# One program instead of two phases: the projection and linear attention of tiles 1 to 8 run as steps beside the expert gathers, with input weights streamed per batch

## The reference, cut to what matters

```python
h = rmsnorm(x, g_norm1); z = h @ w_in
gq, gk, gv, gg, glr, fq, fk, fv, ff = jnp.split(z, _split_points(), axis=-1)
log_a = log_sigmoid(glr @ w_gla_a2 + b_gla_a) / 16
o_gla, S_new = gla_recurrence(gq, gk, gv, log_a, S0)      # linear attention, 4 heads
o_gla = rmsnorm(o_gla, g_gla_onorm) * silu(gg)
o_fox = fox_attention(rmsnorm(fq), k_all, v_all, c_all, P) # softmax attention, 8 heads
x = x + concat[o_gla, o_fox] @ w_out
h = rmsnorm(x, g_norm2)
# PEER: per token and head the best 16 of 128 x 128 experts by two sub-key scores
a = gelu(einsum('nhkd,nd->nhk', peer_u[idx], h))
x = x + einsum('nhk,nhkd->nd', softmax(top) * a, peer_v[idx])
```

## Time and profile before

| | us |
|---|---|
| median of 3 runs | 3622.26 |
| lowest and highest | 3621.23, 3624.48 |
| the profiled execution, span | 3627.2 |
| phase one, to the start of phase two | 0 to 610 |
| first dot product of a gathered row | 693.1 |
| last slots | 3618 |

### The profile page before, as it was taken

The page is one execution under the profiler, slowest core; times in us unless marked ns, Lnnn a source line. Parts: engine busy times, 40 slices in busy tenths (PEclk is TensorE's granted clock), DMA queues, the critical chain, the costliest instruction groups (busy, mean ns, idle before and its releaser), DMA issues.

```text
span 3627.2 us, 32138 instructions
## 1 busy us (share of the span) xinstructions
PE 2778.7 (77%) x8313; PEld 1424.2 (39%) x8313; DVE 2582.2 (71%) x5512; ACT 1483.7 (41%) x3893; POOL 1316.7 (36%) x1154
## 2 busy tenths in 40 slices
PE   7999996677777776777787777677777777787677
PEld 3444445434333343343344343333343333343333
DVE  4333332586886768897786899878777888876786
ACT  2333333244445534444452444444524443343344
POOL 0000001234434444344444444434444543444343
PEclk9999997788888888898888898889988998888889
DMA  4010125799999999999999999999999999999998
GB/s 193 24 47 24 47 100 205 274 420 407 421 399 409 421 421 403 370 413 404 414 420 421 421 408 408 352 421 422 421 421 420 407 414 401 398 404 409 422 420 352
DMA packets 187467, 1267.78 MB, mean 350 GB/s; under 512 B 23508, under 2 KB 24492, under 8 KB 39956
## 3 DMA queue, kind: packets, MB, share of 16 engines
q0 software_dynamic: 159728, 1131.10, 76.3%
q1 hardware_dynamic: 26356, 130.32, 9.0%
q10 hardware_dynamic: 1200, 4.33, 0.3%
HBM read 1238.78 MB, written 26.88 MB: 349 GB/s over the span
## 4 chain that ended last, share of the span: by engine, by line
DMA 33%; PE 20%; DVE 15%; issue 9%; ACT 4%; POOL 2%; DVEq 0%; SPq 0%; ACTq 0%; POOLq 0%
DMA w_in<-in_peer_uv,expert_index 33%; PE ps_acc L1530 13%; DVE w_in L1701 6%; DVE v_sums L1709 3%; PE ps_scores L1506 3%; POOL w_in L1193 2%; PE ps_scores L1386 1%; ACT coef_diag L1360 1%; PE ps_scores L1474 1%; ACT gelu_u_dot_h L1355 1%; DVE key_top_index L1608 1%; DVE key_scores_rest L1609 1%; PE ps_fox_o L1404 1%; DVE key_top_index L1617 1%; DVE expert_top_index L1608 1%
## 5 line engine op out<-in xcount | busy, mean ns | idle before, releaser
L1530 PE MATMUL ps_acc<-w_in,coef_diag 128*128 128x512 f32 x2676 | 1535.2, 716 | 733.0 <-ACT coef_diag L1360 708.2
L1193 POOL DMA_INDIRECT w_in<-in_peer_uv,expert_index x1056 | 1264.7, 1198 | 1667.1 <-PE ps_acc L1530 1466.9
L1701 DVE CUSTOM_DVE_ANT_0 w_in<-w_in 128x1024 f32<-128x1024 f32 x1056 | 1285.7, 1220 | 457.6 <-DMA w_in<-in_peer_uv,expert_index 448.0
L1530 PEld LDWEIGHTS ps_acc<-w_in,coef_diag 128*128 128x128 f32 x2676 | 558.5, 223 | 1514.1 <-ACT coef_diag L1360 972.1
L1355 ACT ACTIVATE gelu_u_dot_h<-u_dot_h 128x2 f32<-128x2 f32 x528 | 107.1, 203 | 1312.7 <-DVE u_dot_h L1701 1299.5
L1709 DVE SCALAR_TENSOR_TENSOR v_sums<-w_in,coefficients,v_sums 128x1024 f32<-128x1024 f32 x387 | 495.7, 1281 | 12.7 <-ACT coefficients L1362 12.3
L460 PE MATMUL ps_z<-w_in,x_T 128*128 128x512 f32 x864 | 407.7, 622 | 6.4 <-DVE w_in L782 6.4
L1506 PE MATMUL ps_scores<-w_in,rows_T 128*128 128x256 f32 x1152 | 263.1, 382 | 0.7 <-issue 0.7
L1360 ACT ACTIVATE coef_diag<-coef_diag,gelu_u_dot_h 128x128 f32<-128x128 f32 x669 | 253.1, 398 | 17.5
L1506 PEld LDWEIGHTS ps_scores<-w_in,rows_T 128*128 128x128 f32 x1152 | 221.2, 192 | 62.7 <-issue 35.7
L460 PEld LDWEIGHTS ps_z<-w_in,x_T 128*128 128x128 f32 x864 | 165.3, 199 | 194.5 <-issue 185.1
(11 more groups left out here) (200 smaller groups left out, 2353.2 us busy)
## 6 DMA issues: line engine op xcount, KB each, us to landing
w_in<-scratch_keys_w SPq DMA_DIRECT2D x48, 1024.0 KB
w_in<-in_w_out_chunks SPq DMA_DIRECT2D x24, 1024.0 KB
w_in<-in_peer_uv,expert_index POOLq DMA_INDIRECT x1056
w_in<-in_w_in_chunks SPq DMA_DIRECT2D x6, 2048.0 KB, 25.0
w_in<-in_w_peer_q_T SPq DMA_DIRECT2D x8, 1024.0 KB, 5.9
scratch_keys_w<-w_in SPq DMA_DIRECT2D x8, 1024.0 KB, 3.9
x_T<-in_x_T POOLq DMA_DIRECT2D x9, 512.0 KB, 4.5
x_rows<-in_x_rows POOLq DMA_DIRECT2D x9, 512.0 KB, 5.2
```

What stands on the lines that cost most here:

```text
L1193: pool.indirect_dma_start(out=ring[:, s % RING, :], out_offset=None, in_=dram["uv"], in_offset=bass.IndirectOffsetOnAxis(ap=idx[:, t % IDX ...
L1530: mm = pe.matmul(acc[:, c, :], diag[:, r, :], ring[:, r, D + c * 512:D + (c + 1) * 512], start=first, stop=False, skip_group_check=True)
L1701: dve.tensor_tensor_reduce(out=ring[:, s % RING, 0:D], in0=ring[:, s % RING, 0:D], in1=h2[:, t % 2, :], scale=1.0, scalar=0.0, op0=ALU.mul ...
```

## The change

The two functions become one, `stream`. Batches are 0, 1-2, 3-4, 5-6, 7-8. On each engine the front of a batch now begins with `mix_front` (projection of its tiles, two tiles to each weight chunk, and the gates) and `gla` (linear attention of one tile, 14 steps, 12 for the sample), ahead of `attend`. The rest of the front and the back stay, but for names.

- w_in is no longer kept. Its twelve half chunks of 256 columns (1 MB) are streamed in every batch, ahead of w_out's and keys_w's, through two buffers (`WBUF = 2`). g_norm1 is multiplied into the turned rows of x instead of into w_in.
- q, k, v, the gates and the linear attention's output stay in SBUF; k, v and log gates are stored as outputs by SyncE and no longer read back. One tile of 5440 columns is shared by linear attention, softmax attention and routing (GpSimd clears it once).
- Folding of the keys is 32 pieces, one in each step of tile 0's linear and softmax attention. Its results are stored in 16 halves; w_q lies in the ring meanwhile, so GpSimd waits for all foldings before the first gather.
- VectorE's copy of h is single: `reopen(t)` stands at the first slot of tile t, not four slots before.
- The front has 1799 steps (1551 before), 108 of them ahead of slot 0 (78). VectorE has 394 of the adds (387).
- The scratch for GpSimd's descriptors is 4096 bytes instead of the default.

`front_plan` gives the new steps the weights in the diff. The slots over which its table spreads a part:

| part | before | change |
|---|---|---|
| rest of routing 0 | 0-40 | 0-17 |
| projection of a batch's tiles | phase one | 18-55, 181-242, 419-479, 676-737 |
| linear attention of a batch | phase one | 55-67, 243-262, 480-500, 737-756 |
| attention 1; 2 | 41-59; 136-161 | 68-76; 76-87 |
| attention 4; 7; 8 | 346-386; 644-705; 875-949 | 287-314; 757-799; 800-845 |
| routing of two tiles | 232-344, 473-586, 744-873 | 104-181, 341-418, 599-676, 872-1040 |

```diff
+BATCHES = [[0], [1, 2], [3, 4], [5, 6], [7, 8]]
+NB = max(len(ts) for ts in BATCHES)
+PLACE = {t: (bi, i) for bi, ts in enumerate(BATCHES) for i, t in enumerate(ts)}
+CW = 2 * DKEY
+PAIRS = 6
+QK, VV, FK, FV, FQ, GG = range(PAIRS)
+IN_CH = 2 * PAIRS
+OUT_CH = D // CW
+CHUNKS = IN_CH + OUT_CH + PH
+WBUF = 2
...
-def mix_phase(nc, ctx, io, dram, shared):
...
+def gla_at(ts):
+    return len(ts) + 1 + IN_CH * len(ts) + 2
+
+
+def gla_steps(t):
+    return 7 + len(levels(t))
+
...
+def front_plan():
...
+    for ts in BATCHES:
+        n = len(ts)
+        weight += [0.6] * (n + 1) + [3.7] * (IN_CH * n) + [0.6] * 2
+        on_pe += [True] * gla_at(ts)
+        for t in ts:
+            weight += [1.1] * gla_steps(t)
+            on_pe += [False] * gla_steps(t)
+        for t in ts:
+            weight += [(13.0 + 7.5 * min(t, TILES - 0.5)) / ATT_STEPS] * ATT_STEPS
+        weight += [3.5] * (OUT_CH * n) + [1.5] * (out_steps(ts) - OUT_CH * n)
+        base = len(weight)
+        on_pe += [True] * (base - len(on_pe))
+        due += [(base, SLOTS * t - 12) for t in ts if t]
+        weight += [0.45] * route_steps(ts)
+        on_pe += [False] * route_steps(ts)
...
-BATCHES = [[0], [1], [2, 3], [4, 5], [6, 7], [8]]
...
-WBUF = 3
...
+        def turned_rows(bi, ts):
+            if bi:
+                sp.wait_ge(s_mm, units_before(bi))
+            for i, t in enumerate(ts):
+                sp.dma_start(xT[i][:].rearrange("p k t -> p (k t)"), dram["xT"][t]).then_inc(x_in[i], 16)
...
+                turned_rows(bi, ts)
+                sp.dma_start(g1[:], dram["g1"]).then_inc(g1_in, 16)
+                sp.dma_start(w_small[:].rearrange("p k n -> p (k n)"), dram["w_in_small"]).then_inc(g1_in, 16)
+                chunk(bi, 0)
+            else:
+                chunk(bi, 0)
+                turned_rows(bi, ts)
+            rows(bi, ts)
+            for c in range(1, IN_CH):
+                chunk(bi, c)
+                if bi == 0 and c == 3:
+                    sp.dma_start(subkeys, dram["subkeys_T"].rearrange("p a k -> p (a k)")).then_inc(sub_in, 16)
+                if bi == 0 and c >= IN_CH - PH:
+                    h = c - (IN_CH - PH)
...
+            for c in range(IN_CH, IN_CH + WBUF):
+                chunk(bi, c)
+            if bi == 0:
+                sp.wait_ge(past_sp, SPLIT)
+                sp.dma_start(dram["negc_past"], past_parts[:]).then_inc(past_st, 16)
+                for x in range(2 * PH):
+                    sp.wait_ge(f_ev, 2 * (x + 1))
+                    sp.dma_start(dram["keys_w"][x // 2][:, x % 2 * D:(x % 2 + 1) * D], folded[x % 2]).then_inc(f_st[x % 2], 16)
+            stores(ts)
+            if TILES in ts and ts[0] != TILES:
+                cache()
+            for c in range(IN_CH + WBUF, IN_CH + OUT_CH + WBUF):
...
+        pool.wait_ge(f_mm, FOLDS)
         load_sums(0)
...
+        def mix_front(bi, ts):
+            n, t0 = len(ts), ts[0]
+            for step in range(gla_at(ts)):
...
+                u = step - (n + 1)
+                if 0 <= u < IN_CH * n:
+                    c, i = divmod(u, n)
+                    pair, half = divmod(c, 2)
+                    q = PAIRS * t0 + pair * n + i
+                    chunk = CHUNKS * bi + c
+                    if i == 0:
+                        pe.wait_ge(wb_in[chunk % WBUF], 16 * (chunk // WBUF + 1))
+                    if u == 0:
+                        wait(pe, s_ev, units_before(bi))
+                    if half == 0:
+                        wait(pe, z_ev, q - 2)
+                    lo = 512 * (q % 3) + CW * half
+                    for k in range(KD):
+                        mm = pe.matmul(S[:, lo:lo + CW], xT[i][:, k, :], wb[chunk % WBUF][:, k * CW:(k + 1) * CW],
+                                       start=(k == 0), stop=(k == KD - 1), skip_group_check=True)
+                    mm.then_inc(z_mm, 1)
...
         def front():
             for bi, ts in enumerate(BATCHES):
+                yield from mix_front(bi, ts)
+                for t in ts:
+                    yield from gla(bi, t)
                 for t in ts:
                     yield from attend(t)
                 yield from project(bi, ts)
...
-
-                dve.wait_ge(f_st[1], 16 * (PH // 2))
-            dve.scalar_tensor_tensor(out=h2[:, b, :], in0=sums[:, b, :], scalar=hrs[:, t:t + 1], in1=g2[:],
+                dve.wait_ge(f_st[0], 16 * PH)
+            wait(dve, dotted, SLOTS * t)
+            dve.scalar_tensor_tensor(out=h2[:], in0=sums[:, b, :], scalar=hrs[:, t:t + 1], in1=g2[:],
                                      op0=ALU.mult, op1=ALU.mult).then_inc(h_r, 1)
 
         def back():
             for s in range(NS + DRAIN):
                 t, i = divmod(s, SLOTS)
-                if s == 0:
-                    reopen(0)
-                if i == SLOTS - 4 and t < TILES:
-                    reopen(t + 1)
                 if s < NS:
+                    if i == 0:
+                        reopen(t)
                     g, n = divmod(s, GRP)
...
-    nc = bacc.Bacc("TRN2", target_bir_lowering=False, num_devices=1)
+    nc = bacc.Bacc("TRN2", target_bir_lowering=False, num_devices=1, dynamic_dma_scratch_size=4096)
```

1533 lines of the change are left out of this document (720 added, 813 removed).

## The result

| | before | the change |
|---|---|---|
| median of 4 runs, us | 3621.74 | 3526.06 |
| lowest and highest | 3618.79, 3624.48 | 3518.32, 3528.73 |
| ratio, 95% interval | | 0.9727 (0.9715 to 0.9739) |
| profiled execution, span | 3627.2 | 3522.1 |
| first dot product of a gathered row | 693.1 | 191.5 |

A forecast was written before the change was run, and what follows sets the result against it. The prediction took data to bound the gathers, at a 421.5 GB/s ceiling, with VectorE nearly the bound in routing. 3627 - 475 + 97 + 166 = 3415, less 5 for the median: 3410 us, forecast range 3330 to 3500.

The forecast's parts named there:

- The head: Before the first dot product of a gathered row: only tile 0 is mixed there, 218 us in place of 693, -475 us.
- The bytes: Beside the gathers: net 40.9 MB more, paid at a ceiling of 421.5 GB/s, +97 us.
- Linear attention: Four stretches beside the gathers: 28 steps of 2.9 us, 80 us against 57 of data; loss 66 us in all.
- the deepest dip: Sign: data rate dips at the four linear-attention stretches, the first the deepest, at 250 to 350 GB/s.
- Routing: Three two-tile stretches: 228 us of VectorE work at 94% share, 243 us against 224 of data; loss 57 us in all.
- term 3: Denser front work in the gather gaps: stalls in routing, linear attention, softmax attention and projection, +166 us, bounds 60 and 380.
- Softmax attention of tiles 1 and 2: In 19 slots beside the gathers: 75 us against 47 of data, 28 us lost.
- Projection: Tiles 1 and 2: 142 us of TensorE against 127 of data, 15 lost; nothing if activity releases the clock.
- Data alone binds: Rival: the ring covers the bursts, term 3 is only 20 us, time 3264 us; chance 0.18.
- Slower than before: Rival: mixing of tiles 1 to 8 does not overlap with the gathers, 3733 us; chance 0.08.
- heavier stalls, still faster: Rival: late hand-overs in front steps hold dot products behind them, term 3 doubles or worse, 3500 to 3615 us; chance 0.14.
- VectorE's waits for landings: Sign: VectorE's waits for gathered rows fall well below 448 us; if they do not fall, the prediction is wrong.

The follow-up runs named there:

- half: The change with only half of each w_in chunk loaded for tiles 1 to 8, 25.2 MB less, work unchanged: 3480.15 us, ratio 0.9595.
- gla2: The change with linear-attention steps weighed 2.0 instead of 1.1 in the plan, so more slots for them: 3500.26 us, ratio 0.9652.
- before_lag4: The kernel before with 8 steps instead of 4 between a routing unit's scores and VectorE's search: 3603.53 us, ratio 0.9934.
- lag4: The change with 8 steps instead of 4 between a routing unit's scores on TensorE and VectorE's search: 3471.35 us, ratio 0.9562.
- pe0: The change with no adds on VectorE in the slots of routing and linear attention, lead still 4 steps: 3437.32 us, ratio 0.948.
- lag4_pe: lag4 with no adds on VectorE in the slots of routing and linear attention, 119 adds moved to TensorE: 3376.53 us, ratio 0.9327.
- att_w: lag4 with softmax attention weighed 26 + 6t a tile instead of 13 + 7.5t, 26 slots for tiles 1 and 2: 3442.82 us, ratio 0.9494.
- lag8_gla: The change with 8 more steps of lead between scores and VectorE's search and linear attention weighed 1.7: 3422.77 us, ratio 0.9437.
- best2: lag4_pe with linear attention weighed 1.6, softmax attention 20 + 6.5t, routing 0.52, plan margin 6 instead of 12: 3296.1 us, ratio 0.9107.
- best1: lag4_pe with linear attention weighed 1.6, routing 0.5 and plan margin 6 instead of 12: 3309.44 us, ratio 0.9117.
- all4: The change with 8 more steps of lead, linear attention weighed 1.7, softmax attention 26 + 6t, plan margin 6 instead of 12: 3433.19 us, ratio 0.9477.
- all5: all4 with no adds on VectorE in the slots of routing and linear attention: 3367.67 us, ratio 0.9283.

## Why the prediction was right and wrong

- **The head (right, size too large).** 191.5 us for 218. Windows over it, from the first chunk on: the twelve chunks, linear attention, softmax attention, and the rest to the first dot product:

```profile
17.00:85.00 68.00, 56.18 (x229) 45.35 (x228) 8.37 (x37) 15.33 (x24) 0.00 (x0) 0.90 0.85 331
85.00:110.00 25.00, 23.18 (x212) 21.01 (x212) 15.57 (x42) 16.21 (x34) 0.00 (x0) 1.00 0.40 160
110.00:141.00 31.00, 26.60 (x193) 22.65 (x192) 3.23 (x10) 16.72 (x44) 0.00 (x0) 0.93 0.43 170
141.00:191.50 50.50, 31.93 (x120) 25.62 (x120) 19.85 (x69) 9.82 (x27) 8.06 (x9) 0.80 0.60 215
```

  The chunks took 68 us instead of 72. Linear attention of tile 0 took 25 us, not 39: TensorE is busy 23 of them, so its steps hardly wait. Attention 0 took 31 (35), and from there it was 50.5 us instead of 57.5.
- **The bytes (right).** 42 MB for 40.9 and a ceiling still at 421 to 422 GB/s. half shows that they are paid only where data binds. By the share of 358 GB/s that the Trainium skill (DMA: Bandwidth & Descriptors, Specifications) gives, the term would by estimate have been 17 us dearer; half of the stretches here run above 390 GB/s.
- **Linear attention (right).** 81, 80 and 77 us for 80, and 73 for 67; 70 us of loss for 66. gla2 shows the mechanism by removing it. The first stretch was not the deepest dip, as the prediction had it: softmax attention of tile 1 was, at 166 GB/s.
- **Routing (the step that failed).** It is the sentence on VectorE's share in term 3: "VectorE ran at 88% with little loss; I give it 94% at best: 243 us." Its work was forecast well (228 us; 232 to 236 measured), its share was not: 86 to 89% and 264 to 271 us, three times. Its loss was put at 57 us for the three stretches and is 137. I read the 88% as a load that data happened to limit. before_lag4 shows what it was: 27 us of waiting for scores in a ring of dependences, mostly free as long as data was longer. Once the stretch was packed, those waits lay on the path. The trace of before had them: the same list of VectorE's groups that gave has this line, with the idle time before it and what ended it, and the prediction makes nothing of it.

```profile
L1604 DVE MAX8 key_top<-key_scores 128x8 f32<-128x128 f32 x32 | 7.8, 284 | 27.0 <-ACT key_scores L1308 27.0
```

  lag4 removed the wait and reached 91% in the stretch shown, still short of the 94. pe0 and lag4_pe show the other half, that VectorE was full, and priced it at 89 to 95 us.
- **Softmax attention of tiles 1 and 2 (mechanism right, size off).** 96 us for 75, 51 lost for 28. att_w shows that six more slots fit into this time; what sets its length stays open, since it ran from 77 us (lag8_gla) to 102 (gla2) with the same 18 slots.
- **Projection (mis-sized by what was left out).** For tiles 1 and 2 the 15 us of loss came out as forecast, TensorE 97% busy, but in 125 us and with fewer bytes, so the agreement is partly luck. The granted clock was 0.95 in it. The recorded text calls TensorE in the gathers of before mostly waiting; by the earlier trace rows it was busy 2181 of 2925 us. By the rule of the Trainium skill (TensorE: Matmul & The Clock Gate, Part 1) that activity releases the clock the item was to vanish: the clock rose as it says, and the loss stayed. The three later projections lose 31 us together and were costed at nothing, as were the 13 us of routing 0, packed from 41 into 18 slots, the 18 us of the last routing, and what the softmax attention of the later tiles lost on top of before.
- **Slips in the sum (luck).** The three routing stretches of the kernel before had lost 47 us already, and these are in the 3627 us; the prediction adds the 57 us of the new ones whole, where by its own working the routing adds 10. Without this the forecast would have been 47 us lower and the miss larger. Its "90 MB of data, 224 us" do not fit each other: 90 MB are 214 us at the ceiling, but the stretch moved 264 x 357 = 94 MB, so the 224 us are right. The rest of 109 us in VectorE's work holds the 9.1 us of accumulator reads that its 1.6 us a slot hold too.
- **The rivals.** Data alone binds fell with the first routing window (357 GB/s). Slower than before decides at a term 3 of 378 us, and 297 were measured. The time lies inside 3290 to 3590, but above the forecast's own 3330 to 3500, where the rival "heavier stalls, still faster" (3500 to 3615) stands, which had 0.14. Its mechanism, a late hand-over that holds what stands behind it, is the wait that lag4 removed; its size, term 3 doubled or worse, was not reached (1.8 times), and the fullness of VectorE, the other half, was not in it.
- **The signs that were named.** In routing the rate is below 400 GB/s as named, VectorE's share is not the 92%. GpSimd's waits for ps_acc turned longer ( 1466.9 us, longest 9.2; now 1807.1, longest 12.6). TensorE waits 11.0 us for w_in's chunks in all, 10.6 of it in the head, as costed. VectorE's waits for landings were to fall well below the 448 us and fell to 412.8 only: there are none in the routing of tiles 1 and 2, but 67.5, 65.0 and 62.2 us in the projections of the three later pairs of tiles, where VectorE has little else to do. I had named that as a sign that I am wrong.

What stays open: why linear attention of the first pair still loses 25 us in best2, when it loses 10 in best1 with one slot more and 10 in gla2 with three more, and how much of each gain is the clock's and how much the chain's; nothing here holds the clock while the load changes.

## What to carry to other kernels

An engine's busy share in a stretch that something else bounds is not its limit. Before packing the stretch, look at what ends its idle time: a wait on a product that itself stands behind this engine's own output, in an in-order queue, can become the bound as soon as the cover goes. Here four more steps of lead took 57 us of loss out of routing.

When a plan spreads work by weights, edits that win one by one need not add up: all4 holds more of them than lag8_gla and is 10 us slower. How much a plan is worth also depends on the load under it: the plan of all4 won 38 us over lag4 and, as all5, 9 over lag4_pe. The plans of best1 and best2, which give routing 81 to 83 slots instead of 74, won 67 to 80 over lag4_pe; what they give with VectorE full was not run, so it is not shown that the order, first relieve and then tune, is what mattered.
